# First z group begun tile by tile, and mLSTM state numerators as pairs of 64-row tiles

## The reference, cut to what matters

```
h = x * (1 + scale1) + shift1          # shift, scale from SiLU(cond) @ w_mod + b_mod
z = h @ w_in                           # 1024 -> 5 column groups: u | q,k,v,o of the mLSTM | gates | attention
inter = exp(b + m - m_t)               # per token, head and direction
num = (s @ v) + inter * (q @ C)        # C: 64 x 64 state of the chunk, one extra column gives q @ n
den = sum(s) + inter * (q @ n)
h_m = num / max(|den|, exp(-m_t))
```

## Time and profile before

| | us |
|---|---|
| runs of the kernel, median (lowest, highest) | 3178.14 (3174.45, 3179.07) |
| the profiled execution | 3172.86 |
| its span | 3171.0 |
| PE busy in the span | 3022.0 (95%) |
| DVE busy | 1921.2 (61%) |
| ACT busy | 994.5 (31%) |
| mean granted clock of TensorE | 0.974 |

### The profile page before, as it was taken

One profiled execution on the slowest core, in us unless ns is written; L12 is line 12 of the kernel. 1 busy time (PEld: TensorE's weight loads), 2 busy tenths in 40 slices (PEclk: granted clock), 3 DMA queues, 4 the chain that ended last, 5 costly groups with the idle time before them and its releaser, 6 DMA issues.

```text
span 3171.0 us, 43665 instructions
## 1 busy us (share of the span) xinstructions
PE 3022.0 (95%) x16241; PEld 2527.9 (80%) x16241; DVE 1921.2 (61%) x3490; ACT 994.5 (31%) x1914; POOL 402.7 (13%) x581
## 2 busy tenths in 40 slices
PE   5999979999899999999979998999989999999998
PEld 4788855568898999988968887555779998899997
DVE  4437677754766777667474577677456444544447
ACT  3212335444412222122353233445262221222212
POOL 1002333321000000000030033434010000000002
PEclk7999989999999999999989999999999999999999
DMA  5431220002222233222121012100211111101112
GB/s 223 157 116 40 72 90 0 0 27 70 80 67 74 87 94 106 67 73 87 54 94 59 31 49 78 44 0 14 84 41 41 53 41 40 54 30 51 44 37 73
DMA packets 93846, 201.46 MB, mean 64 GB/s; under 512 B 12432, under 2 KB 13088, under 8 KB 93024
## 3 DMA queue, kind: packets, MB, share of 16 engines
q1 hardware_dynamic: 78240, 151.76, 14.7%
q0 software_dynamic: 15424, 47.25, 4.4%
HBM read 181.88 MB, written 17.08 MB: 63 GB/s over the span
## 4 chain that ended last, share of the span: by engine, by line
PE 62%; issue 24%; DVE 6%; DMA 2%; ACT 2%; DVEq 1%; POOL 1%; ACTq 1%; POOLq 0%; SPq 0%
PE ps L1866 14%; PE ps L1870 14%; PE ps L1869 14%; PE ps L2086 6%; PE ps L2057 3%; PE ps L2076 2%; PE ps L2077 2%; DVE nm L1536 2%; DMA w_raw<-in_w_slots 1%; PE ps L1984 1%; DVE w_lo L509 1%; DMA modw<-in_w_mod 1%; PE ps L1979 1%; DMA w_raw<-in_m_slots 1%; PE ps L1848 1%
## 5 line engine op out<-in xcount | busy, mean ns | idle before, releaser
L1866 PE MATMUL ps<-hi,w_hi 128*128 128x384 f32 x1584 | 536.2, 339 | 21.2 <-DVEq L447 9.9
L1869 PE MATMUL ps<-lo,w_hi 128*128 128x384 f32 x1584 | 534.1, 337 | 0.0
L1870 PE MATMUL ps<-hi,w_lo 128*128 128x384 f32 x1584 | 534.0, 337 | 0.0
L504 ACT CAST w_hi<-w_raw 128x512 fp32r<-128x512 f32 x368 | 215.0, 619 | 728.1 <-PE ps L1866 680.5
L1866 PE MATMUL ps<-w_hi,hi 128*128 128x512 f32 (+1 forms) x1008 | 388.5, 385 | 4.9 <-ACT stg L832 3.0
L1870 PE MATMUL ps<-w_hi,lo 128*128 128x512 f32 (+1 forms) x1008 | 380.3, 377 | 0.0
L1869 PE MATMUL ps<-w_lo,hi 128*128 128x512 f32 (+1 forms) x1008 | 380.1, 377 | 0.0
L1695 DVE TENSOR_TENSOR ps<-ps,gate 128x512 f32<-128x512 f32 x288 | 201.0, 698 | 240.3 <-PE ps L1870 240.1
L1866 PE MATMUL ps<-w_hi,f_hi 128*128 128x512 f32 x864 | 336.6, 390 | 0.0
L1870 PE MATMUL ps<-w_hi,f_lo 128*128 128x512 f32 x864 | 336.5, 389 | 0.0
L1869 PE MATMUL ps<-w_lo,f_hi 128*128 128x512 f32 x864 | 336.4, 389 | 0.0
(11 more groups left out here) (311 smaller groups left out, 4809.7 us busy)
## 6 DMA issues: line engine op xcount, KB each, us to landing
w_raw<-in_w_slots SPq DMA_DIRECT2D x368, 256.0 KB, 3.2
w_raw<-in_m_slots SPq DMA_DIRECT2D x160, 256.0 KB, 2.9
out<-xr POOLq DMA_DIRECT2D x18, 512.0 KB, 3.2
modw<-in_w_mod SPq DMA_DIRECT2D x4, 2048.0 KB, 15.9
acc<-in_x_in SPq DMA_DIRECT2D x3, 1536.0 KB, 22.4
zq_dram<-stg POOLq DMA_DIRECT2D x18, 256.0 KB, 2.4
xr<-in_x_in POOLq DMA_DIRECT2D x2, 2304.0 KB, 9.3
xr<-out POOLq DMA_DIRECT2D x2, 2304.0 KB, 9.7
```

Of the source, the lines that this page charges most:

```text
L504: act.copy(w_hi[:, j, :], w_raw[:, j % RAW, :]).then_inc(S["w_hi_done"], 1)
L1866: mm = pe.matmul(out, a_hi, b_hi, start=first, stop=False)
L1869: pe.matmul(out, a_hi, b_lo, start=False, stop=False)
L1870: return pe.matmul(out, a_lo, b_hi, start=False, stop=last)
```

## The change

In layer 0, the tokens are turned, modulated and multiplied tile by tile. TensorE turns tiles 0 and 1 ahead and tile t + 2 before the product of tile t, into two pairs of banks in turn (4, 5 and 6, 7); the product of tile t waits for its own low half alone. The barrier is gone; POOL waits for the modulation products instead. The gate products go behind tile 2, behind tile 5 and before tile 8, all into bank 2, and ScalarE copies each out with its own semaphore count. The 24 modulation slots go behind the tiles 0 to 5, into bank 3; VectorE's rows and columns of them stand in its tile loop. SP loads the first four weight slots before the fourth modulation buffer, and the token tiles 3 to 8 behind the slots 4 to 7. VectorE splits slots 0 to 3 before the last modulation chunk and slots 4 to 7 behind its half of tile 0. Layer 1 keeps its order.

In the numerators, each of the eight products reads the 64 rows of its head alone. Pairs of heads lie on rows 0 to 63 and 64 to 127 and write the banks 6 and 7; both directions lie in one bank, and VectorE reads a direction across both banks.

```diff
+T_BANKS = ((4, 5), (6, 7))
+G_BANKS = ((2, 2, 2), (4, 5, 6))
...
 sp.dma_start(condt[:], cond).then_inc(S["const_ld"], 16)
-for n in range(NCH):
+def mod_chunk(n):
     sp.dma_start(modw[n][:], w_mod[n]).then_inc(mod_w_ld[n], 16)
+for n in range(NCH - 1):
+    mod_chunk(n)
 def x_rows(j):
 for i, (kind, n) in enumerate(RING):
-    if i == 0:
+    if i == RAW:
+        mod_chunk(NCH - 1)
         x_rows(0)
-    if i == RAW:
+    if i == SLOTS:
         x_rows(1)
...
     if not L:
-        phase(pool)
+        pool.wait_ge(S["mod_ps"], NCH * KT)
+        pool.drain()
+        own(pool)
     else:
...
-    if L == 0:
-        act.wait_ge(S["mod_col"], NCH)
-    for t in range(NT) if not L else ():
-        n, u = 2 * NT * L + t, t % 3
-        act.wait_ge(S["xT_ps"], n + 1)
-        act.wait_ge(S["h_done"], START + n - 2)
+    def modulated_first(t):
+        u = t % 3
+        act.wait_ge(S["xT_ps"], t + 1)
+        act.wait_ge(S["h_done"], START + t - 2)
-            act.activation(hf[:, u, kt * P:(kt + 1) * P], ps[:, 2 * u + 1, (kt % 4) * P:(kt % 4 + 1) * P], ACT.Identity,
+            act.activation(hf[:, u, kt * P:(kt + 1) * P], ps[:, T_BANKS[t % 2][1], (kt % 4) * P:(kt % 4 + 1) * P], ACT.Identity,
-        hi_of(t, hf[:, u], n)
-        if not L and t in (2, NS - 1):
-            split_hi(act, 0, 0, None, range(RAW) if t == 2 else range(RAW, SLOTS))
+        hi_of(t, hf[:, u], t)
-        phase(act)
-    def gate_rows():
-        act.wait_ge(S["ml_ld"], 32 * L + 32)
-        act.copy(selr[:], selc[:])
-        act.wait_ge(S["row_ld"], 16 * L + 16)
-        act.wait_ge(S["y_rdy"], NT * L)
-        for g in range(3):
-            act.wait_ge(S["g_ps"], 3 * L + g + 1)
-            act.activation(ri[:, g * GRP:(g + 1) * GRP], ps[0:ROWS, 4 + g, 0:GRP], ACT.Identity, bias=rcon[:, 0:1])
-            ins = act.activation(rf[:, g * GRP:(g + 1) * GRP], ps[64:64 + ROWS, 4 + g, 0:GRP], ACT.Identity, bias=rcon[:, 1:2])
-        ins.then_inc(S["gr_done"], 1)
-    if not L:
-        gate_rows()
+        split_hi(act, 0, 0, None, range(RAW))
+        act.wait_ge(S["mod_col"], NCH)
+        modulated_first(0)
+        split_hi(act, 0, 0, None, range(RAW, SLOTS))
+        modulated_first(1)
+        modulated_first(2)
+    def gate_rows(g):
+        if g == 0:
+            act.wait_ge(S["ml_ld"], 32 * L + 32)
+            act.copy(selr[:], selc[:])
+            act.wait_ge(S["row_ld"], 16 * L + 16)
+            act.wait_ge(S["y_rdy"], NT * L)
+        act.wait_ge(S["g_ps"], 3 * L + g + 1)
+        act.activation(ri[:, g * GRP:(g + 1) * GRP], ps[0:ROWS, G_BANKS[L][g], 0:GRP], ACT.Identity, bias=rcon[:, 0:1])
+        act.activation(rf[:, g * GRP:(g + 1) * GRP], ps[64:64 + ROWS, G_BANKS[L][g], 0:GRP], ACT.Identity,
+                       bias=rcon[:, 1:2]).then_inc(S["gr_done"], 1)
...
             act.wait_ge(y_st[t // 3], 16 * 3 * L)
-        if L and t == 3:
-            gate_rows()
+        for g in range(3) if L and t == 3 else ():
+            gate_rows(g)
         z_tile(L, 0, t, z[:, t, ZUG:ZUG + 256], ps[:, t % 2, 0:256])
+        if not L and t + 3 < NT:
+            modulated_first(t + 3)
+        if not L and t in (2, 5, NT - 1):
+            gate_rows(t // 3)
     act.wait_ge(S["abs_row"], L + 1)
...
 for m in range(NCH):
+    if m == NCH - 1:
+        split_lo(dve, 0, 0, range(RAW))
     mod_rows(m, 6)
...
             low(2 * NT * L + t - 1, t - 1, hf[:, (t - 1) % 3])
-        if t in (2, NS - 1):
-            split_lo(dve, 0, 0, range(RAW) if t == 2 else range(RAW, SLOTS))
+        else:
+            split_lo(dve, 0, 0, range(RAW, SLOTS))
+        if t in (3, 5, 7):
+            mod_rows(NCH + t // 2 - 1, 3)
+        if t in (4, 6, 8):
+            mod_columns(NCH + t // 2 - 2, 3, GRP)
     if not L:
         low(2 * NT * L + NS, NS, hf[:, NS % 3])
-        phase(dve)
     def modulation(c, part):
...
-    for part in range(3):
-        modulation(0, part)
-    dve.wait_ge(S["gr_done"], L + 1)
+    dve.wait_ge(S["gr_done"], 3 * L + 3)
...
         v = lambda b: ps[:, b, 0:2 * PV].rearrange("p (a b) -> p a b", b=VE)
+        pairs = ps[:, 6:8, 0:2 * PV].rearrange("p e (d a b) -> p d a e b", d=2, b=VE)
         for d in range(2):
-            dve.tensor_tensor(hn[:, d], v(6 + d), b2(cols[:, n, 2, d], VE), ALU.mult)
+            dve.tensor_tensor(hn[:, d].rearrange("p (a e) b -> p a e b", e=2), pairs[:, d],
+                              b2(cols[:, n, 2, d].rearrange("p (a e) -> p a e", e=2), VE), ALU.mult)
         dve.drain()
...
-    for t in range(NT) if not L else ():
+    def first_turned(t):
-        if t > 2:
-            pe.wait_ge(S["hi_done"], t - 2)
+        if t == 1:
+            pe.wait_ge(S["mod_col"], NCH)
+        if t > 1:
+            pe.wait_ge(S["hi_done"], t - 1)
-            mm = pe.transpose(ps[:, 2 * (t % 3) + k // 4, (k % 4) * P:(k % 4 + 1) * P], acc[:, t, k * P:(k + 1) * P], ident[:])
+            mm = pe.transpose(ps[:, T_BANKS[t % 2][k // 4], (k % 4) * P:(k % 4 + 1) * P], acc[:, t, k * P:(k + 1) * P], ident[:])
+    def gates(g):
+        pe.wait_ge(S["h_done"], START + 2 * NT * L + 3 * g + 3)
+        if not L and g:
+            pe.wait_ge(S["gr_done"], g)
+        a = slice(g * GRP, (g + 1) * GRP)
+        for k in range(KT):
+            if L and g == 0:
+                pe.wait_ge(S["w_lo_done"], slot(L, 0, k) + 1)
+            mm = product(ps[:, G_BANKS[L][g], 0:GRP], w_hi[:, k, 256:384], w_lo[:, k, 256:384], hi[:, k, a], lo[:, k, a],
+                         k == 0, k == KT - 1)
+        mm.then_inc(S["g_ps"], 1)
-        phase(pe)
+        for t in range(2):
+            first_turned(t)
-    for g in range(3):
-        if L:
-            pe.wait_ge(S["h_done"], START + 2 * NT * L + 3 * g + 3)
-        a = slice(g * GRP, (g + 1) * GRP)
-        for k in range(KT):
-            if g == 0:
-                pe.wait_ge(S["w_lo_done"], slot(L, 0, k) + 1)
-            mm = product(ps[:, 4 + g, 0:GRP], w_hi[:, k, 256:384], w_lo[:, k, 256:384], hi[:, k, a], lo[:, k, a],
-                         k == 0, k == KT - 1)
-        mm.then_inc(S["g_ps"], 1)
+        for g in range(3):
+            gates(g)
+    def first_modulation(t):
+        i, at = t // 2, t % 2 * 4
+        if i and not at:
+            pe.wait_ge(S["mod_col"], NCH + i)
+        if i < 3:
+            mod_slots(NCH + i, range(at, at + 4), 3)
-        if not here or t == 0:
+        if not here or t == 0 or c == 0:
...
         for d, s_ in enumerate((n, NS - 1 - n) if n < NS else (NT, NT)):
-            for h in range(MH):
-                pe.matmul(ps[:, 6 + d, h * VE:(h + 1) * VE], qbd[:, h // 2, h % 2], cs[:, s_, d, h // 2], start=True, stop=True)
+            for p_ in range(2):
+                for e in range(2):
+                    a, o = slice(HD * e, HD * e + HD), (2 * d + p_) * VE
+                    pe.matmul(ps[:, 6 + e, o:o + VE], qbd[a, p_, e], cs[a, s_, d, p_], start=True, stop=True)
         pe.wait_ge(S["m_sw"], START + NT * L + n + 1)
...
             bank = x % 2 if s_ < 0 else 1 if s_ < NT or not t else t % 2
+            if not (L or c):
+                if t == NT - 1:
+                    gates(2)
+                if t + 2 < NT:
+                    first_turned(t + 2)
+                pe.wait_ge(S["h_done"], START + t + 1)
             pe.wait_ge(S["z_done"], START + 45 * L + x - (1 if s_ < 1 or s_ > NT + 2 else 0))
                 pe.wait_ge(S["gm_done"], NT * (L + 1))
-            dense(L, c, t, bank, W if c else 256, c and t == 0, t == NT - 1, S["z_ps"])
+            dense(L, c, t, bank, W if c else 256, (c or not L) and t == 0, t == NT - 1, S["z_ps"])
+            if not (L or c):
+                if t in (2, 4, 6):
+                    mod_turn(NCH + t // 2 - 1, 3, GRP)
+                if t in (2, 5):
+                    gates(t // 3)
+                if t < 6:
+                    first_modulation(t)
             modulation(c, t)
```

More of the change, by code:

```diff
@@ L1141, in mod_rows, with mod_columns @@
                 ins.then_inc(S["mod_row"], 1)
-            def mod_columns(m, bank):
+            def mod_columns(m, bank, at=0):
                 k, c = kind_of(m), m % NCH
@@ L1148, in mod_columns @@
                     o = 32 * k + 8 * j + c
-                    src = ps[:, bank, 32 * j:32 * j + 2]
+                    src = ps[:, bank, at + 32 * j:at + 32 * j + 2]
                     if j < 2:
@@ L1165, in modulate1 @@
                 for kt in range(KT // 2):
-                    ins = dve.tensor_scalar(hf[:, u, kt * P:(kt + 1) * P], ps[:, 2 * u, kt * P:(kt + 1) * P],
+                    ins = dve.tensor_scalar(hf[:, u, kt * P:(kt + 1) * P], ps[:, T_BANKS[t % 2][0], kt * P:(kt + 1) * P],
                                             col(L, 0, 1, kt, int(t < NS)), col(L, 0, 0, kt, int(t < NS)), ALU.mult, ALU.add)
@@ L1850, in mod_slots, with mod_turn @@
                     mm.then_inc(S["mod_ps"], 1)
-            def mod_turn(m, bank):
+            def mod_turn(m, bank, at=0):
                 pe.wait_ge(S["mod_row"], m + 1)
```

(2 more changed lines are left out.)

## The result

The changed kernel takes 3155.22 us (median of 4 runs, 3151.15 to 3157.48), the kernel before 3177.89 beside it. The ratio is 0.9936, with a 95% interval from 0.9922 to 0.9949, that is 20 us less, between 16 and 25. The forecast was 3156. The sum came out right, its terms did not: the head gave more than forecast, the numerators less, and two things took time back, one that was costed at nothing and one that stood in no term.

The account below looks back on a forecast made before the run. TensorE's chain was taken to bound the kernel. Head 13.8 plus numerators 8.4 made 22.2 us off the profiled 3172.86, giving 3150.7; with the median 5.3 higher, 3156 was expected, range 3146 to 3170.

Parts of the forecast that it names:

- The start of the first tile: Layer 0 head: first projection product starts at 44 us, against 63.3 before.
- From there to the end of the ninth tile: Layer 0, first column group: 58.0 us from first product, ending at 102.0 against 115.84; gain 13.8 us.
- modulation pieces: Layer 0 head: 24 modulation slots between the tiles, four in 1.28 us less a tail, 7.5 us in all.
- the slow clock: Layer 0 head: the first 5 us of products run at half the clock, adding 2.5 us.
- the transposes: Layer 0 head: seven blocks of eight transposes between the tiles, about 1.0 us each, 7.0 us.
- the changes of shape: Layer 0 head: changes of array shape around the modulation slots, about 0.2 us each, 1.2 us.
- The upper bound: Head's gain: 17 us, ending at 98.8, with 0.6 us of waits and shape changes free; 18 if the clock rises earlier.
- Rivals 2 and 3: Rival 2: first group keeps waits or loses clock, 3163, chance 0.12; rival 3: 1.2 GHz throughout group, 3192, chance 0.03.
- The gate rows "at nothing": Step into group 1: third gate block's copies delay VectorE's row computation 1 to 2 us, costed at nothing.
- The numerators: mLSTM state numerators: paired 64-row products overlap on the array's halves, gaining 0.7 us a block, 8.4 us in all.
- Six blocks a layer: mLSTM: of nine numerator blocks per layer, six count on the chain, excluding blocks 1, 4 and 9; 12 in all.
- rival 4: First tile held until 57 us, head gains 0 to 1; 3178 with pairs not overlapping, 3170 if overlapping; chance 0.05.

Follow-up runs that it names:

- early rows: Changed kernel with ScalarE's copies of the third gate block between the two halves of the slot splits opening group 1: 3151.7 us, ratio 0.9924.
- the clock held: Changed head with 128-row numerators and 24 unread products before block 1, 3154.53 us, ratio 0.9935, set against the same filling with paired numerators.
- head alone: Changed kernel with the numerators of before (eight 128-row products, one bank per direction) and VectorE's old read of them: 3157.06 us, ratio 0.995.
- numerators alone: Kernel before, with its old head, given the paired 64-row products and VectorE's read of them: 3167.8 us over 11 runs, ratio 0.9985.
- second trace of the changed kernel: Trace from running the changed kernel again, unedited, as a yardstick in the second group: 3153.66 us, ratio 0.9931.
- filling: Changed kernel plus 24 products with unread results before the wait for weights in block 1 of each layer: 3142.63 us, ratio 0.9903.
- all tiles turned first: Changed kernel with all nine token tiles transposed and modulated before the first product, rest of the change kept: 3162.79 us, ratio 0.9965.

## Why the prediction was right, and where its terms were wrong

**The start of the first tile: right.** 44 us forecast, 44.07 measured, by the path that was worked out: last modulation load 29.2 (29.48), VectorE free of the weight differences of slots 4 to 7 at 41.2 (41.5), then VectorE's two pieces. That TensorE wouldn't wait for a DVE queue there was wrong only in the words: it waits 4.4 us for VectorE's low part itself, which was in the 44.

**From there to the end of the ninth tile: 4.2 us too long.** Forecast 58.0, measured 97.83 - 44.07 = 53.8. The tiles (9 x 2.87) and the gate blocks (12.5) stand. Too dear were the six modulation pieces, 7.5 against 6 x 0.99 = 5.9; the slow clock, 2.5 against 1.6; the waits, 1.5 against 0.9; and the transposes, 7.0 against 5.1. Of the transposes two errors add up. A block costs 0.85, since the 1.09 of the timeline has a tail that the next product overlaps. And only six blocks lie between the first product and the end of the ninth tile: tile t + 2 is turned before the product of tile t, so the third tile's transposes (38.60) fall into the wait for the first tile's low part, where they cost nothing. That sum, 25.8 + 12.5 + 5.9 + 5.1 + 1.6 + 0.9, is 51.8. The other 2.0 us are what the forecast had at 1.2, the changes of shape: a tile behind transposes takes 2.95 to 3.05 in place of 2.87, and the turns of the modulation rows come to it. The errors are of two kinds, then: durations taken with their tails where the distance between starts is what counts, and one block counted on the chain that lies in a wait. The upper bound, 17 to 18, was the better value, but its working isn't all there: the terms shown, with 0.6 us of waits and no price for the shapes, give 99.9 and not 98.8.

**Rivals 2 and 3: refuted.** The clock is at 1.00 between the tiles, transposes and modulation pieces included; in no trace of a kernel with this tile order is it lower from 50 us to the row transposes near 148. The Trainium skill says in TensorE: Matmul & The Clock Gate, section on PE-mode transpose, that transposes don't count as busy for the clock in the way that products do. With 0.85 us of transposes between tiles of 2.9 us no row here shows the rule at work: the clock stayed at 1.00.

**The gate rows "at nothing": wrong by 1.1 us.** The cover was said to be that TensorE wants the result only after seven tiles of group 1. But VectorE does its work in order, and behind the row computation stands the modulation row, which TensorE's modulation product wants much earlier. A move that delays one item of a queue delays all behind it; the forecast named the wrong first reader. The early rows show this step alone.

**The numerators: the mechanism right, the net per block 0.56 and not 0.7.** The block is shorter by 1.73 - 1.04 = 0.69. The forecast's own terms, 0.9 for the pairs and 0.2 for two changes of shape, give 1.1 a block and so a gain of 0.63 (with its 1.08, 0.65); the 0.7 was rounded up, which alone is 0.6 to 0.8 us of the 1.6 missing over twelve blocks. The dense product before it and the value products after it are dearer by 0.08 and 0.05: changing the array's shape costs at the neighbours too. Six blocks a layer gave 21.9 - 18.5 = 3.4 and 22.5 - 19.1 = 3.4, so 6.8 for the forecast 8.4, with the blocks that count as they were named (block 1, block 4 and the last gave nothing). The parts by themselves are in line with it: 5 (2 to 8) alone, 4 to 6 on top of the head, 7 to 10 with the clock held.

**What was in no term: the clock behind an idle stretch.** Block 1 was rightly put down as waiting for VectorE, and so as worth nothing. It took more: the products after the wait run at 1.2 GHz, before the change too, and 10 to 14 us of it in the profiled run against 7 cost 1.6 and 2.5 us. The head alone shows the same loss and the numerators alone don't, and one and the same kernel has 7 and 10 us in one trace, 10 and 14 in another. So a difference of this size is chance between executions, as is the 3.2 us gained at the row transposes, where the second trace of the changed kernel has the lower clock again. Whether the head shifts the odds isn't settled: in the seven traces with the changed head and no filling (all tiles turned first among them) the stretch is 7 us four times, 10 us nine times and 14 us once, in the two with the old head it is 7 us all four times. What is shown is that the low stretch goes when the idle time goes.

So the forecast of 22.2 us became 21.6 by +4.5 up to the second tile of group 1 (18.3 for 13.8), -1.1 for the gate rows, -1.6 for the numerators, -4.1 and +3.2 for the clock, and -1.5 in small pieces. The errors cancelled: that the median lies 1 us from the forecast is luck, and what was right is the path to the first tile, the halves that overlap and the count of blocks. The head measures between 15.7 and 18.3 us in the traces that hold it, at the upper end of its bounds of 5 to 18. A slip that changed nothing stands in rival 4: with the pairs not overlapping its terms give about 3180, not 3178.

## What to carry to other kernels

Cost a moved piece by the distance between starts in the timeline, not by its duration, and for every queue it passes ask who reads the next item in it, not only who reads this one. Where an engine that runs at a clock level waits in front of short products, price the slow products behind the wait too, and try products without a reader in the gap: here 24 of them, 3.1 us of work in a gap that was idle anyway, gave 6 to 10 us, where the paired numerators gave 4 to 10, and twelve of them gave nothing that could be measured. Small products that leave half of the array's rows idle are worth pairing if the two halves stand close to each other in the program, one by one or two by two. And ask of every piece that you add up whether it lies on the chain or in a wait.

## What the hardware did that I had not expected

- Passes of 64 rows start out of program order across the two halves, by the pattern of their starts: with eight passes on one half and eight behind them for the other, the second half began while the first still had three passes to start. The gain depends on how far apart they stand: 1.04 us in turns, 1.09 two by two, 1.53 eight by eight.
- At block 1, idle stretches of 1.5 to 3.3 us ahead of 65-column products were followed by the lower clock, which stayed for 7 to 14 us; at block 1 of layer 0 TensorE was busy for 11.00 of 11.00 us of it.
- Its length differs between executions of the same kernel (7 and 10 us against 10 and 14), which moves a profiled run by 2 to 4 us: a term of that size read from one pair of traces isn't settled by them.
